# Hybrid trunk on Trainium2: convolution and query norms two groups sooner, one low part in four steps, and a new order in the attention stage

## What is computed

```python
for l in range(DEPTH):
    h = rms_norm(x, attn_norm[l])
    proj = h @ w_in[l]
    (gq, gk, gv, gz, gb, ga, nq, kcmp, vcmp, kslc, vslc, kwin, vwin, ngate,
     cb, cc, cx) = jnp.split(proj, split_at, axis=-1)
    ...
    o_gdn = gated_delta_rule(...)             # 4 heads of 64, recurrence over the tokens
    o_nsa = nsa_attention(nq, kcmp, vcmp, kslc, vslc, kwin, vwin, ngate, cos, sin, ...)
    o_conv = cb * causal_depthwise_conv(cc * cx, conv_w[l])
    x = x + concatenate([o_gdn, o_nsa, o_conv]) @ w_out[l]
    h2 = rms_norm(x, ffn_norm[l])
    gate, up = jnp.split(h2 @ w_gate_up[l], 2, axis=-1)
    x = x + (jax.nn.silu(gate) * up) @ w_down[l]
```

## Time and profile before

| what | value |
|---|---|
| median of three runs | 1396.84 us (1394.92 to 1398.08) |
| profiled execution, time | 1394.56 us |
| its span, first to last instruction | 1392.8 us |
| mean granted TensorE clock | 0.999 of full |
| PE busy | 1363.6 us (98%) |
| DVE busy | 626.1 us (45%) |
| ACT busy | 507.4 us (36%) |
| POOL busy | 618.1 us (44%) |

### The profile page before, as it was taken

One profiled execution on the slowest core, in us unless ns is written; L12 is line 12 of the kernel. 1 busy time (PEld: TensorE's weight loads), 2 busy tenths in 40 slices (PEclk: granted clock), 3 DMA queues, 4 the chain that ended last, 5 costly groups with the idle time before them and its releaser, 6 DMA issues.

```text
span 1392.8 us, 19856 instructions
## 1 busy us (share of the span) xinstructions
PE 1363.6 (98%) x8298; PEld 1164.8 (84%) x8298; DVE 626.1 (45%) x1022; ACT 507.4 (36%) x872; POOL 618.1 (44%) x327
## 2 busy tenths in 40 slices
PE   7999999999999999999999999998999999999998
PEld 6998977789888888888879999776998888888887
DVE  5638577723333213442165386766144432133421
ACT  5564335624323212222336542456242222123210
POOL 4457326633334444443344663356334434434442
PEclk9999999999999999999999999999999999999999
DMA  7326310024343234333222532100233332343222
GB/s 180 104 71 138 88 32 1 2 56 75 96 111 96 83 93 112 91 91 114 84 91 65 129 106 61 31 2 2 61 91 91 92 110 86 100 110 92 91 84 83
DMA packets 182219, 114.76 MB, mean 82 GB/s; under 512 B 46193, under 2 KB 169329, under 8 KB 182129
## 3 DMA queue, kind: packets, MB, share of 16 engines
q1 hardware_dynamic: 180016, 113.22, 29.2%
q10 hardware_dynamic: 2112, 0.26, 0.1%
HBM read 109.80 MB, written 3.67 MB: 81 GB/s over the span
## 4 chain that ended last, share of the span: by engine, by line
PE 87%; DVE 6%; SPq 2%; issue 2%; ACT 1%; POOL 1%; DMA 0%; DVEq 0%; ACTq 0%
PE ps L621 72%; PE ps L926 2%; PE ps L731 2%; PE ps L985 2%; DVE att L1943 1%; PE ps L909 1%; PE ps L883 1%; SPq L329 1%; DVE st L272 1%; PE ps L657 1%; PE ps L711 1%; DMA w_raw<-in_w_in 0%; PE ps L961 0%; PE ps L762 0%; DVE state L1970 0%
## 5 line engine op out<-in xcount | busy, mean ns | idle before, releaser
L1448 POOL TENSOR_TENSOR w_lo<-w_raw,w_hi 128x2048 fp32r<-128x2048 f32 (+1 forms) x100 | 452.8, 4528 | 623.1 <-ACT w_hi L1126 566.0
L1126 ACT ACTIVATE w_hi<-w_raw 128x2048 fp32r<-128x2048 f32 (+1 forms) x100 | 188.6, 1886 | 560.1 <-PE ps L621 550.8
L621 PE MATMUL ps<-hT_hi,w_lo 128*128 128x512 f32 x928 | 231.1, 390 | 0.0
L621 PE MATMUL ps<-hT_hi,w_hi 128*128 128x512 f32 x896 | 224.5, 392 | 0.9 <-DVE hT_lo L1567 0.5
L621 PE MATMUL ps<-hT_lo,w_hi 128*128 128x512 f32 x896 | 222.7, 390 | 0.0
L621 PEld LDWEIGHTS ps<-hT_hi,w_lo 128*128 128x128 f32 x928 | 173.5, 188 | 36.0 <-issue 0.3
L621 PEld LDWEIGHTS ps<-hT_lo,w_hi 128*128 128x128 f32 x896 | 167.8, 188 | 34.9 <-issue 0.3
L621 PEld LDWEIGHTS ps<-hT_hi,w_hi 128*128 128x128 f32 x896 | 166.4, 188 | 36.0 <-DVE hT_lo L1567 1.3
L1995 DVE TENSOR_TENSOR aT_lo<-ffn_tmp,aT_hi 128x512 fp32r<-128x512 f32 x44 | 142.0, 3228 | 30.7 <-ACT aT_hi L1136 30.7
L2062 DVE TENSOR_TENSOR ffn_tmp<-ps,ffn_tmp 128x512 f32<-128x512 f32 x44 | 30.4, 692 | 243.7 <-ACT ffn_tmp L1420 243.7
L621 PE MATMUL ps<-w_hi,aT_hi 128*128 128x512 f32 (+1 forms) x544 | 123.1, 353 | 0.0
(11 more groups left out here) (315 smaller groups left out, 1684.7 us busy)
## 6 DMA issues: line engine op xcount, KB each, us to landing
w_raw<-in_w_gate_up SPq DMA_DIRECT2D x88, 512.0 KB, 5.1
w_raw<-in_w_in SPq DMA_DIRECT2D x20, 1024.0 KB, 5.5
w_raw<-in_w_down SPq DMA_DIRECT2D x16, 1024.0 KB, 5.0
w_raw<-in_w_out SPq DMA_DIRECT2D x32, 256.0 KB, 4.3
w_raw<-in_w_down SPq DMA_DIRECT2D x8, 768.0 KB, 4.5
w_raw<-in_w_in SPq DMA_DIRECT2D x2, 1120.0 KB, 5.5
w_raw<-in_w_in SPq DMA_DIRECT2D x2, 1056.0 KB, 7.3
x_tok<-in_x SPq DMA_DIRECT2D x4, 512.0 KB, 5.4
```

The costliest lines, as they stand in the source:

```text
L621: mm = nc.tensor.matmul(out_ap, a(ab, k), b(bb, k), start=first and i == 0, stop=last and i == len(kts) - 1)
L1126: nc.scalar.activation(whi[:, c % 2, 0:kt * w], raw[:, c % 2, 0:kt * w], ACT.Copy).then_inc(S["w_hi"], 1)
L1448: nc.gpsimd.tensor_tensor(wlo[:, c % 2, 0:kt * w], raw[:, c % 2, 0:kt * w], whi[:, c % 2, 0:kt * w].bitcast(F32), ALU.subtract).then_inc(S ...
```

## The change

Six edits, in both layers.

1. VectorE: `short_conv(1)`, `q_norm(2)` and `q_norm(3)` move to n = 31. `conv_gate(33)` moves from step k = 0 of the loop to behind `rope`.
2. TensorE: `query_transposes(0)` comes ahead of the unrotated transposes; ScalarE: `query_hi(0)` ahead of `unroped_T(0)`.
3. VectorE: `query_lo(1)` moves from behind `maximum(0)` to ahead of the loop.
4. The mask additions are made for bank 7 first; `recur_first(0)` waits for two of them (`cadd` 2), not four.
5. ScalarE: `mix_hi` moves ahead of `exp(k, 0)`.
6. GpSimd: the low part of chunk 12, made in one step ahead of the attention, is made in four of a quarter each behind `scale_probs(8)` to `scale_probs(11)`.

```diff
@@ tensor_layer
-            for t in range(NT):
+            def unroped_transposes(t):
                 pe.wait_ge(*S.at("qn", t + 1, l))
                 for m in range(4):
...
                 else:
-                    pe.wait_ge(*S.at("cadd", 4, l))
+                    pe.wait_ge(*S.at("cadd", 2, l))
...
-            for m in range(3):
+            query_transposes(0)
+            for t in range(NT):
+                unroped_transposes(t)
+            for m in (1, 2):
                 query_transposes(m)
@@ scalar_layer
+            query_hi(0)
             unroped_T(0)
             unroped_T(1)
-            query_hi(0)
...
+                if k % 6 == 5 and k >= 11:
+                    mix_hi((k - 11) // 6)
                 if k < N_SLOTS:
                     exp(k, 0)
                 if 0 <= k - LAG_TRANSPOSE < N_SLOTS:
                     evacuate(k - LAG_TRANSPOSE)
-                if k % 6 == 5 and k >= 11:
-                    mix_hi((k - 11) // 6)
@@ pool_layer
+            def split_lo_quarter(c, i):
+
+                if i == 0:
+                    pool.wait_ge(*S.at("w_hi", c + 1, l))
+                kt, w = chunk_shape(c)
+                part = slice(i * kt * w // 4, (i + 1) * kt * w // 4)
+                ins = nc.gpsimd.tensor_tensor(wlo[:, c % 2, part], raw[:, c % 2, part],
+                                              whi[:, c % 2, part].bitcast(F32), ALU.subtract)
+                if i == 3:
+                    ins.then_inc(S["w_lo"], 1)
...
-            split_lo(12)
             pool.wait_ge(*S.at("roped", 1, l))
...
                 scale_probs(k)
+                if 8 <= k < 12:
+                    split_lo_quarter(N_IN, k - 8)
@@ vector_layer
-                if n in (30, 32):
-                    g = (n - 30) // 2
+                if n in (30, 31):
+                    g = n - 30
                     dve.wait_ge(*S.at("ev_dve", g + 7, l))
                     short_conv(g)
                 if n == 30:
                     q_norm(0)
-                if n >= 32:
-                    q_norm(n - 30)
+                if n == 31:
+                    q_norm(2)
+                    q_norm(3)
...
             dve.nop().then_inc(S["roped"], 1)
+            conv_gate(len(GROUPS) - 1)
...
-                    for b in range(2):
+                    for b in (1, 0):
...
             key_lo(1)
+            query_lo(1)
...
-                if k == 0:
-                    conv_gate(len(GROUPS) - 1)
-                    query_lo(1)
```

## The result

The changed kernel takes **1388.66 us** (median of 4 runs, 1387.9 to 1389.6) against 1396.45 us for the kernel before beside it (4 runs, 1394.92 to 1398.08): ratio 0.994, 95% interval 0.9928 to 0.9952, so 7.8 us or 0.56% less. The prediction was 1390.0 in a range of 1387.2 to 1393.8. The profiled execution has a span of 1387.4 us, 5.4 less than the 1392.8 of before.

The account below looks back on a forecast made before the run. TensorE, busy in 98% of the span, bounds the kernel, so only its idle time can be won. Start 1.4 plus tail 2.0 make 3.4 us a layer, 6.8 for both: 1396.84 to 1390.0 us, range 1387.2 to 1393.8.

Parts of the forecast that it names:

- Start: Start of the attention stage: score step 0 0.95 us sooner, score step 1 another 0.43 us; 1.4 us a layer.
- The cover: VectorE's queue at the stage start: rotation done 2 us before TensorE wants it, key transposes with over 2 us.
- Mask additions: First recurrence step: its 0.7 us wait goes, but TensorE waits later at 212.0; 0, with 0.7 us as other end.
- Quarters: GpSimd behind scaling steps 8 to 11: each quarter of 1.16 us fits the idle times; cost 0.
- Tail: Steps 17 and 23, scaling 18 and output transposes: 2.0 us a layer, with 1.2 and 2.3 us as ends.
- Steps 17 and 23: TensorE's product step no longer waits for the mix's low part on VectorE: 0.60 us at each step.
- the output transposes: End of the tail: the 0.28 us wait ahead of them shifts away too; 0.25 us.
- Scaling 18: GpSimd's scaling ends at 270.8 instead of 271.98, so TensorE's 0.56 us wait for it goes: 0.55 us.
- (a): Rival: start gains, tail does not, another input being as late; 2.8 to 5.2 us gained, about 1393; chance 0.23.
- (c): Rival: unrotated copies on ScalarE cost 0.3 us more each, tail lost; under 2.8 us left, about 1395; chance 0.11.
- (b): Rival: mask additions pay and the second query block's new wait is hidden; 9.0 us gained, 1387.9; chance 0.08.
- (d): Rival: GpSimd's queue, steps 8 to 12; quarters of q us cost 4q - 13.6 a layer; 1399.6 at 4.6; chance 0.03.

Follow-up runs that it names:

- start_only: Edits 1 to 3 alone against the kernel before (edits 4 to 6 undone): 1393.36 us, ratio 0.9985.
- best: Changed kernel with output copies ahead at k = 3, 5, 8, 14, 20, 23, compressed copy ahead at 8, step 23's low part ahead, step 3's maximum reordered: 1380.26 us.
- best_no_mask: best with edit 4 undone (mask additions in their old order, the recurrence waiting for all four): 1379.81 us.
- late4: Changed kernel with four more VectorE products of 128x512 behind the moved short convolution in each layer: 1388.63 us.
- late4_whole: late4 with edit 6 undone (chunk 12's low part in one step again, ahead of the attention): 1394.69 us.
- whole_low: Changed kernel with edit 6 undone (chunk 12's low part whole again, ahead of the attention): 1388.54 us.
- mix_only: Edit 5 alone (the mix's high part ahead of the first exponential) against the kernel before: 1391.36 us, ratio 0.9967.
- quarters4: Changed kernel with every quarter of chunk 12's low part made four times, 5.25 us instead of 1.28: 1407.17 us.

## Why the prediction held, point by point

- **Idle time of TensorE is what the change can win, and it reaches the end one for one.** Held: PE busy is the same to 0.2 us, and 3.12 us a layer give the change of span less the 0.85 us that were lost at 41 us.
- **Start, 1.4 us forecast.** Measured 1.48 (1.40 in start_only): score step 0 0.96 us sooner (0.95 forecast), step 1 another 0.52 (0.43), with the new wait of 0.36 for ScalarE that was forecast at 0.4. The cover was sized at 2 us for the rotation and is 3.0; the order within VectorE's queue (copies for the key transposes, gate, rotation) came as written.
- **Mask additions, 0.** Held, and by the mechanism given: the wait went to the next block that needs VectorE, 0.62 us. best and best_no_mask, made to expose a gain, did not.
- **Quarters, 0 in time.** The time held; a quarter took 1.27 to 1.28 us and not 1.16. The reason was incomplete: I asked only what GpSimd's new steps do in their new place and not what the old step would do in its old place once VectorE's work is moved beside it. It would have held the convolution up by 2.95 us, and late4 against late4_whole prices that at 6.1 us where the cover is used up. I had cited the Trainium skill's rule on contention for the quarters, and the rule that stands next to it (quoted at whole_low) was the one to ask about the step that was taken away.
- **Tail, 2.0 us.** Measured 1.63 in mix_only. Steps 17 and 23 gave 0.68 and 0.67 (0.6 each) and the output transposes 0.22 (0.25). Scaling 18 gave 0.33, not 0.55: that term was mis-sized. It took for granted that only GpSimd held the block up. GpSimd was early enough, but ScalarE's copy out of bank 5, which stands behind its exponential, ended at 270.30 and held the second three transposes until 270.41; the block takes 1.16 us where the one at 274.07 takes 0.82, and in best, with this copy moved ahead, it takes 0.82. And at step 23 0.24 us were lost that no step of mine had: the maximum of step 23 stands on VectorE behind the low part of the gated output, which waits for ScalarE (277.40, then 278.01), a chain that starts with the exponential of step 22 and moved less than TensorE did, so the transposes' wait grew from 0.90 to 1.14. "The next two groups of pieces shift too" looked at GpSimd alone.
- **The sum.** 3.4 against 3.12 a layer, 6.8 against 6.2: by the stage the forecast is 0.6 us too high, by the medians (7.8) 1.0 too low. The interval of the medians' gain is 6.7 to 10.1 us (0.9928 and 0.9952 of 1396.45). Of the 1.3 us between 1388.66 and 1390.0, 0.4 is the median before (1396.45 and not 1396.84), and no term explains the rest. So how near the total came says little of the terms; what speaks for them are the waits.
- **The rivals.** (a) and (c) did not come: the tail paid. (b) had both of its conditions fail. (d) is real as a mechanism and far away (q = 1.28 against 4.25), and its price was wrong in both parts: fewer waits, and the clock on top.

## What to carry to other kernels

When work is moved on VectorE, read what GpSimd does in the *new* place, not only the queues behind it: a 0.48 us instruction took 3.43 beside a GpSimd step, and nothing showed it in the total because there was cover for it. A wait that a reorder removes is worth only what the next wait behind it leaves; undo each edit by itself, and also with the cover taken away, before calling it useless. And look for copies that stand behind an instruction whose input comes later: taking such copies, and two other steps like them, forward was worth more (8.4 us) than the change itself (7.8 us).

## What the runs showed of the hardware that was not expected

- A VectorE TENSOR_SCALAR of 128x512 from SBUF to SBUF beside a GpSimd TENSOR_TENSOR that had begun before it: 3.43 us instead of 0.48, ending 0.28 us after GpSimd's step (whole_low; 3.43 and 3.44 us in start_only and late4_whole). GpSimd's step took 4.58 us with and without it.
- The other way round, in the kernel before: a GpSimd TENSOR_TENSOR of 128x32 takes 0.25 us at 171.61, where VectorE's steps read PSUM, and 0.72 at 173.03, beside VectorE's SCALAR_TENSOR_TENSOR of 172.89, which has two operands in SBUF and keeps its 1.54 us for two.
- TensorE's granted clock, 1.00 in every stretch of the changed kernel's attention stages, fell to 0.50 in quarters4: in layer 0 after an idle time of 2.2 us, staying there through the next of 3.1 until 262; in layer 1 it was at 0.50 behind each of the two and at 1.00 between them. It cost 3.7 and 4.5 us more than the waits themselves.
- TensorE's second weight load of a block starts 0.11 to 0.12 us after the end of the copy that it waits for, and the profile marks this wait as "issue", without a releaser (the blocks of 1.03 and 1.16 us).
- GpSimd's subtraction of a quarter (128x512 to fp32r) takes 1.27 to 1.28 us against 1.16 for its product of the same size, and four quarters 5.1 us against 4.58 for the whole.
